# Expert weights in transfers of 2 MB and gathered rows three experts ahead, in a decoder layer with a mixture of experts

## The reference

```python
def run(args):
    xi, e = args
    a, b = jnp.split(xi @ w_gu[e], 2, axis=-1)
    return (jax.nn.silu(a) * b) @ w_down[e]
...
yb = lax.map(run, (xb, blk_exp)).reshape(P, D)
return jax.ops.segment_sum(yb * buf_gate[:, None].astype(yb.dtype), buf_tok, num_segments=T)
```

## Time and profile before

| | |
|---|---|
| median of 3 runs | 860.1 us (858.65 to 861.57) |
| the profiled execution's own time | 858.78 us |
| its span | 857.0 us |
| PE busy | 735.6 us, 86% |
| POOL busy | 183.9 us, 21% |
| moved by DMA | 246.52 MB, mean 288 GB/s |
| granted TensorE clock, mean | 0.981 of full |

### The profile page before, as it was taken

The page is one execution under the profiler, slowest core; times in us unless marked ns, Lnnn a source line. Parts: engine busy times, 40 slices in busy tenths (PEclk is TensorE's granted clock), DMA queues, the critical chain, the costliest instruction groups (busy, mean ns, idle before and its releaser), DMA issues.

```text
span 857.0 us, 10224 instructions
## 1 busy us (share of the span) xinstructions
PE 735.6 (86%) x3645; PEld 382.9 (45%) x3645; DVE 205.8 (24%) x573; ACT 148.7 (17%) x363; POOL 183.9 (21%) x188
## 2 busy tenths in 40 slices
PE   6999999999989999689999997877777878777783
PEld 6787688887758445333333332222222222222220
DVE  2422303285768202721011010100100100100120
ACT  5223213106454311110010010000000000000000
POOL 5101000070300000013323323132132132132121
PEclk9999999999998999879999999999999999999997
DMA  9652824020610595559999999999999999999992
GB/s 303 118 152 62 277 104 106 3 75 1 252 45 1 232 424 232 197 203 409 415 407 410 412 406 406 416 414 408 413 416 406 416 413 408 415 415 408 416 414 75
DMA packets 76885, 246.52 MB, mean 288 GB/s; under 512 B 24944, under 2 KB 44303, under 8 KB 52235
## 3 DMA queue, kind: packets, MB, share of 16 engines
q1 hardware_dynamic: 63697, 230.96, 68.1%
q0 software_dynamic: 11776, 8.58, 4.5%
q10 hardware_dynamic: 1378, 6.54, 1.9%
HBM read 239.95 MB, written 24.92 MB: 309 GB/s over the span
## 4 chain that ended last, share of the span: by engine, by line
PE 45%; SPq 29%; DMA 15%; DVE 5%; issue 3%; ACT 2%; POOL 1%; ACTq 0%; POOLq 0%; DVEq 0%
PE bank L1108 42%; SPq L586 20%; DMA reg_b<-in_exp_w_gu 10%; SPq L593 9%; DMA reg_a<-in_exp_w_gu 3%; PE bank L1111 3%; DMA ffn_in<-reg_x 1%; DVE reg_a L1883 1%; DVE reg_y L2093 1%; ACT reg_y L1091 1%; DVE reg_b L1666 1%; DVE small L1843 1%; DVE reg_y L2101 1%; POOL small L691 0%; DVE reg_y L1890 0%
## 5 line engine op out<-in xcount | busy, mean ns | idle before, releaser
L1108 PE MATMUL bank<-reg_w,reg_y 128*64 128x512 f32 (+2 forms) x512 | 136.9, 572 | 15.4 <-DMA reg_w<-in_exp_w_gu 15.4
L1108 PE MATMUL bank<-reg_a,reg_y 128*64 128x512 f32 x528 | 124.3, 607 | 22.6 <-DMA reg_a<-in_exp_w_gu 16.9
L1108 PE MATMUL bank<-reg_b,reg_y 128*64 128x512 f32 x528 | 122.7, 600 | 22.3 <-DMA reg_b<-in_exp_w_gu 16.6
L2097 DVE TENSOR_TENSOR reg_y<-reg_y,bank 128x256 f32<-128x256 f32 x32 | 13.5, 421 | 418.9 <-ACT reg_y L1091 418.9
L1108 PEld LDWEIGHTS bank<-reg_w,reg_y 128*64 128x64 f32 (+2 forms) x512 | 45.4, 144 | 94.9 <-issue 54.1
L1108 PE MATMUL bank<-reg_b,reg_w 128*128 128x260 f32 x384 | 85.3, 383 | 0.0
L1108 PEld LDWEIGHTS bank<-reg_a,reg_y 128*64 128x64 f32 x528 | 34.6, 138 | 103.6 <-issue 50.6
L1108 PEld LDWEIGHTS bank<-reg_b,reg_y 128*64 128x64 f32 x528 | 34.6, 136 | 101.2 <-issue 58.0
L1108 PEld LDWEIGHTS bank<-reg_b,reg_w 128*128 128x128 f32 x384 | 72.7, 190 | 12.0 <-issue 1.1
L1111 PE MATMUL bank<-small,reg_y 128*128 128x128 f32 (+3 forms) x206 | 42.8, 317 | 24.5 <-DVE reg_y L2097 15.0
L1108 PE MATMUL bank<-reg_w,reg_b 128*128 128x256 f32 (+2 forms) x320 | 60.5, 382 | 1.1 <-DVE reg_b L1580 1.1
(11 more groups left out here) (355 smaller groups left out, 649.7 us busy)
## 6 DMA issues: line engine op xcount, KB each, us to landing
reg_a<-in_exp_w_gu SPq DMA_DIRECT2D x44, 1024.0 KB, 27.8
reg_b<-in_exp_w_gu SPq DMA_DIRECT2D x44, 1024.0 KB, 27.6
reg_w<-in_exp_w_gu SPq DMA_DIRECT2D x40, 1024.0 KB, 27.9
reg_a<-in_exp_w_down SPq DMA_DIRECT2D x22, 1024.0 KB, 28.1
reg_b<-in_exp_w_down SPq DMA_DIRECT2D x22, 1024.0 KB, 28.0
reg_h<-in_exp_w_down SPq DMA_DIRECT2D x20, 1024.0 KB, 28.1
reg_w<-in_w_in SPq DMA_DIRECT2D x9, 1024.0 KB, 11.0
reg_w<-in_w_out SPq DMA_DIRECT2D x2, 2048.0 KB, 11.1
```

Of the source, the lines that this page charges most:

```text
L1108: return eng.matmul(out, lhsT, rhs, start=start, stop=stop, skip_group_check=True)
L2097: tt(hid[b], silu[b], bank[2 + b][:, 256:512], ALU.mult).then_inc(S["hid_made"], 1)
```

## The change

`GU_PARTS` goes from 4 to 2: gate and up of an expert come as two transfers of 2 MB, each with a piece of 16 KB for a partition; PE waits and releases by halves. The gathered rows get three buffers instead of two, in reg_x instead of reg_y, with a semaphore each, and are asked for three experts ahead. The counts that PE waits for follow from that. Two semaphores that only order the POOL and PE programs become one.

```diff
-GU_PARTS = 4
+GU_PARTS = 2
...
-        xe_rows = [reg_y.cut(512) for _ in range(2)]
+        xe_rows = [reg_x.t[:, 512 * g:512 * g + 512] for g in range(3)]
...
-        x_gathered = [sem(f"x_gathered{i}") for i in range(2)]
+        x_gathered = [sem(f"x_gathered{i}") for i in range(3)]
...
-            load_gu(2, 2, parts=(0, 1))
+            load_gu(2, 2, parts=(0,))
             eng.wait_ge(bank_full[bank_of["Y3.1"]], turn_of["Y3.1"] + 1)
-            load_gu(2, 2, parts=(2, 3))
+            load_gu(2, 2, parts=(1,))
...
-                eng.indirect_dma_start(xe_rows[e % 2], None, x1_dram, idx, bounds_check=2 * T - 1, oob_is_err=False).then_inc(x_gathered[e % 2], 16)
+                eng.indirect_dma_start(xe_rows[e % 3], None, x1_dram, idx, bounds_check=2 * T - 1, oob_is_err=False).then_inc(x_gathered[e % 3], 16)
...
-                eng.sem_inc(S["gather_asked"], 1)
-                gather(0)
-                gather(1)
+                eng.sem_inc(S["rows_asked"], 1)
+                for e in range(3):
+                    gather(e)
                 for e in range(N_EXP):
-                    if e + 2 < N_EXP:
+                    if e + 3 < N_EXP:
                         eng.wait_ge(S["xe_turned"], n + e + 1)
-                        eng.sem_inc(S["gather_asked"], 1)
-                        gather(e + 2)
+                        eng.sem_inc(S["rows_asked"], 1)
+                        gather(e + 3)
...
-            def turn_tokens(b, gathered):
-                eng.wait_ge(x_gathered[b], gathered)
+            def turn_tokens(g, gathered):
+                eng.wait_ge(x_gathered[g], gathered)
...
-                    turn_tokens(1 - b, gathered)
+                    turn_tokens((g + 1) % 3, gathered)
```

More of the change, by code:

```diff
@@ L423, in layer_kernel @@
             xe_turned xe_made gu_done silu_done hid_made xt_turned hT_made down_done y_copied
-            ffn_in_stored in_slot_made table_made idx_steps idx_made next_at scatter_asked gather_asked round_scattered round_open
+            ffn_in_stored in_slot_made table_made idx_steps idx_made next_at rows_asked round_scattered round_open
             gates_made gates_tabled slot_gates_made x1_stored outputs_done ident_made blocks_zeroed x1_smp""".split()
@@ L765, in _ @@
                 eng.wait_ge(S["idx_made"], r + 1)
-                eng.sem_inc(S["gather_asked"], 1)
-                gather(0)
-                gather(1)
+                eng.sem_inc(S["rows_asked"], 1)
+                for e in range(3):
+                    gather(e)
                 for e in range(N_EXP):
-                    if e + 2 < N_EXP:
+                    if e + 3 < N_EXP:
                         eng.wait_ge(S["xe_turned"], n + e + 1)
-                        eng.sem_inc(S["gather_asked"], 1)
-                        gather(e + 2)
+                        eng.sem_inc(S["rows_asked"], 1)
+                        gather(e + 3)
                     eng.wait_ge(S["y_copied"], n + e + 3)
-                    eng.sem_inc(S["scatter_asked"], 1)
+                    eng.sem_inc(S["rows_asked"], 1)
                     if e:
                         eng.wait_ge(y_scattered[(e - 1) % 2], 16 * N_EXP * r + 32 * ((e + 1) // 2))
-                        eng.sem_inc(S["scatter_asked"], 1)
+                        eng.sem_inc(S["rows_asked"], 1)
                     add_rows(e)
@@ L1505, in gate_table @@
                 ins.then_inc(S["gates_tabled"], 1)
-            def turn_tokens(b, gathered):
-                eng.wait_ge(x_gathered[b], gathered)
-                eng.sem_inc(S["gather_asked"], 1)
-                by_channel = xe_rows[b].rearrange("n (p c) -> n c p", c=4)
+            def turn_tokens(g, gathered):
+                eng.wait_ge(x_gathered[g], gathered)
+                eng.sem_inc(S["rows_asked"], 1)
+                by_channel = xe_rows[g].rearrange("n (p c) -> n c p", c=4)
                 for c in range(4):
@@ L1550, in _ @@
             with eng.Fori(0, rounds) as r:
-                turn_tokens(0, 256 * r + 16)
+                turn_tokens(0, 16 * USES[0] * r + 16)
                 gate_table()
@@ L1555, in _ @@
                         g = j % 3
-                        expert(N_EXP * r + 6 * i + j, j % 2, g, 16 * USES[g] * r + 32 * i + 16 * (j // 3) + 16, 256 * r + 48 * i + 16 * ((j + 1) // 2) + 16)
+                        expert(N_EXP * r + 6 * i + j, j % 2, g, 16 * USES[g] * r + 32 * i + 16 * (j // 3) + 16, 16 * USES[(g + 1) % 3] * r + 32 * i + 16 * ((j + 1) // 3) + 16)
                 for e in range(N_EXP - N_EXP % 6, N_EXP):
@@ L1560, in _ @@
                         slot_table(r + 4)
-                    expert(N_EXP * r + e, e % 2, g, 16 * USES[g] * r + 16 * (e // 3) + 16, 256 * r + 16 * ((e + 1) // 2) + 16 if e + 1 < N_EXP else None)
+                    expert(N_EXP * r + e, e % 2, g, 16 * USES[g] * r + 16 * (e // 3) + 16, 16 * USES[(g + 1) % 3] * r + 16 * ((e + 1) // 3) + 16 if e + 1 < N_EXP else None)
         @block.vector
```

## The result

The changed kernel takes 870.48 us (median of 4 runs, 869.79 to 871.12) where the kernel before takes 859.85 us beside it: a ratio of 1.0125, 95% interval 1.0103 to 1.0146. That is slower by 10.6 us, outside the range given. The profiled execution took 871.12 us, its span is 869.4 us.

What follows compares the result with a forecast made beforehand. The prediction took the weight stream's DMA to bound the experts. Start +1.7, end +1.9 and stream length -4.2 summed to -0.6 us, giving 859.5 us in terms of the median, range 856.0 to 864.5 us.

Steps and rivals of the forecast that it cites:

- What bounds the kernel: Experts' main stretch, 450 to 835 us: the weight stream sets the pace, DMA share 1.02 at 412 GB/s.
- The order of PE and POOL confirms the pace: Experts: PE needs 12.67 us for an early expert with slots filled ahead, 15.95 us for a later one.
- Start of the stream, +1.7: Expert 3's first weights: SP issues later, as the first release comes after half of expert 0's gate and up; +1.7 us.
- End, +1.9: Expert 31: after the last gate and up bytes land, PE has two groups of eight records to multiply, not one; +1.9 us.
- Length of the stream, -4.2: Gate and up of experts 3 to 31: 16 KB pieces save 9.1 ns of overhead per piece dropped; -4.2 us.
- The rule of the Trainium skill: Weight stream: about 3 cycles for a packet would make the saving 1.6 us and the sum +2.0.
- Coarser waits, 0: PE and SP between start and end: waiting and releasing by halves gives the same total wait; 0 us.
- third row buffer, 0: Gathers three experts ahead: PE had no row of a wait for a gather, so nothing to win; 0 us.
- the POOL rival: POOL's scatters land late behind longer pieces and become the bound: +15 us, 875 us, chance 0.08.
- it still fits: POOL's scatter pair: both landed after 13.7 us, by a landing of 11.8 us, against a pair issued every 15.95 us.
- The point given, a landing beyond 14.0 us: One scatter's landing time from which the case of POOL as the bound was said to hold.
- One sign: Gate and up transfers land 30 us or more after issue if SP's queue holds a number of pieces; no time changes.

Runs made afterwards that it cites:

- number 3: The changed kernel with transfers of 2 MB and waits by halves kept, but moved in 8 KB pieces: 863.08 us, ratio 1.0044.
- number 11: A second run of the changed kernel with prompt and sample scatters each waiting only for their own predecessor: 860.81 us, ratio 1.0012.
- number 4: The changed kernel with separate semaphores, so prompt and sample scatters each wait only for their own predecessor: 859.45 us, ratio 0.9990.
- Number 10: The changed kernel, scatters waiting apart, expert 3's first and expert 31's last half of gate and up as two 1 MB transfers each: 856.94 us, ratio 0.9958.
- Numbers 2: The changed kernel with GU_PARTS back at 4 (1 MB transfers), keeping three row buffers and gathers three ahead: 860.16 us, ratio 1.0005.
- number 1: The kernel before with only GU_PARTS = 2 and matching early loads, still two row buffers: 885.03 us, ratio 1.0275.
- number 6: The changed kernel with gate and up as one 2 MB transfer (16 KB pieces) and two of 1 MB (8 KB pieces): 860.43 us, ratio 1.0002.
- number 8: The changed kernel with four 1 MB transfers (8 KB pieces), each sample scatter waiting for its expert's prompt scatter to land: 913.48 us, ratio 1.0621.

## Why the prediction was wrong

**What bounds the kernel** was read right but for one word: "The order of PE and POOL confirms the pace" used the steady 15.95 us only. The 12.67 us of the early experts stood in the same paragraph and were never held against POOL.

**Start of the stream, +1.7.** From PE's begin of expert 0 to SP's first issue it took 5.07 us (371.99 to 377.06), not 3.76: +1.3. Numbers 3 and 11 have +1.4, number 4 only +0.3. About right, slightly over. **End, +1.9.** Down began 5.9 us after the last group instead of 4.2: +1.7. Together 3.0 against 3.6, and number 3 measured 3.2 us with its interval from 2.3 to 5.2.

**Length of the stream, -4.2.** From the first issue for expert 3 to PE's begin on the last half of expert 31, number 4 took 834.95 - 376.03 = 458.9 us, number 11 458.5, and number 3, with short pieces, 837.22 - 375.18 = 462.0: -3.1 and -3.6 for the two. Against the kernel before, whose last quarter PE begins at 837.12 after a first issue at 373.86, it is 463.3 us, so numbers 4 and 11 lie at -4.3 and -4.8. Number 10's whole gain is 3.1 us. So 4.2 was the right size, as far as single profiles tell; the rate came out at 415 GB/s, not 416. The rule of the Trainium skill ("DMA: Bandwidth & Descriptors", "Why small descriptors are slow (HBM only)"), from which the estimate was 1.6 us, lies further off than the line through the rates of 2 and 8 KB pieces, which gave 4.2. With these terms the sum is between -0.1 and -1.8 us, and number 4 measured -0.4 and +0.8.

**Coarser waits, 0, and third row buffer, 0.** Numbers 2 and 3 bear both out, each with the other part as it was. But the buffer's nothing holds for short pieces only: with long ones it is worth 14.5 us (number 1). That PE's turns have no row of a wait for a gather, so that "there is nothing to win", was right of the kernel before, not of the change.

**The step that failed is the POOL rival's "it still fits".** The mechanism stood there, and had 8 chances in 100. Three things in that step were off. First, both scatters were given the landing of 8.8 us, the median over the two kinds; the sample scatter, behind the prompt's pieces, took 9.1 to 9.2 and now takes 13.0 to 13.2, where the step had 11.8. And the step had nothing for the way from the landing to the next scatter, which takes 0.9. The round thus is 1.9 + 13.1 + 0.9 = 15.9 us, not 13.7, and it is measured at 15.85 from expert 11 to 28. The median over both kinds, 11.0 us now, hides this. Second, the step compared this with 15.95 us and called the rest a margin. PE runs at 12.67 us for an expert while the slots are full, and POOL had 16.4 us (387.70 to 486.04 for six experts) against the 12.7 us of before: nearly 4 us lost on each, until PE stood still for its rows. Third, nothing gave it back: with the weights as pace an expert takes 15.87 us (number 4) or 15.84 (number 10), and a chain of 15.85 us has no surplus to catch up with. The lag was 38 us at expert 11 and 35.5 at expert 28. The point given, a landing beyond 14.0 us, was therefore wrong; the point is the pair's time against PE's own pace, and number 6 shows that it need not hurt as long as it is below the weights' time, since the lag is then made up in time.

The rival's price, +15 us for the chain, was not far from what came out as 870.5 - 860.1 = 10.4 us (the changed kernel against the two measurements of number 4), but it was worked out otherwise: 0.7 us lost on each of 29 experts, where it was nearly 4 us on each of the first ones and nothing after. That it lay near is in part luck.

One sign came out as said: transfers of gate and up landed 40.6 us after their issue in number 4, before 27.6, at nearly the same rate. In the changed kernel, where SP waits for PE, it was 28.7 to 30.4.

Not settled: why the round in the steady part is so near to the weights' own. Each prompt scatter there waits for a landing and for nothing else, so the round is the chain's. But the landings themselves grew shorter: on the path that ended last the sample scatters took 14.2, 13.9 and 13.4 us to land at 405 to 439 us and 12.9 to 13.7 later. In number 8 the round was 18.2 us over the first ten experts and 16.8 later. Whether the lag, through the slots, makes the landings shorter was not tried.

## What to carry to other kernels

Here a larger DMA piece in a full stream made the stream of weights 3 to 5 us shorter, and every small transfer beside them slower, by 2 us (prompt scatters) to 4 us (sample scatters and gathers). So before pieces are lengthened, add up the chain of dependent small transfers for one round of the loop, and compare it with the fastest pace that the loop has at any time, not with its average pace. Where such transfers needn't wait for each other, give each kind its own semaphore; and cut only the first and the last transfer finely, where granularity is on the path.

## What the runs showed of the hardware

How long a row transfer takes beside a full weight stream depends on the length of the weight pieces: sample scatters landed after 9.2, 11.3 and 13.1 us with none, 8 and 16 pieces of 16 KB for an engine and expert; 2.7 us was the shortest landing of a scatter. Transfers of 2 MB in 8 KB pieces (9.3 us, number 3) behave like transfers of 1 MB, so it is the piece and not the transfer.

TensorE's granted clock fell from 1.00 to 0.91 in 450 to 835 us when PE began to wait up to 3.9 us for gathers. After a wait of 3.41 us at 801 to 804 us the next five microseconds were granted 0.50 (the level of 1.2 GHz), and the same 16 records of down took 6.02 instead of 3.65 us. In numbers 3 and 4, with the waits by halves, it stayed at 1.00. Number 6 was granted 0.95 in the same stretch, with waits for weights up to 4.0 us, where number 4 had up to 2.6 and 1.00; what exactly the waits must be for the clock to fall was not tried.
